# One hybrid backbone layer on one core: loads and orders of the mixer's pass and first steps rearranged, the first hyena half of the output projection put between the first scores and the first numerators

## The chip, the cores and the metric

The kernel runs on one core of one Trainium2 chip. The metric is the device time of one execution in microseconds, the median of several executions. The core has five engines with queues of their own: PE (TensorE, matrix products), DVE (VectorE), ACT (ScalarE), POOL (GpSimd) and SP (SyncE), which issues all the DMA transfers here. They meet at semaphores only.

## The reference

One layer (DEPTH = 1) over 2048 latent tokens and 256 context tokens of width 1024. A modulated, normalised input is projected; one half of the width feeds a bidirectional mLSTM with 4 heads of 128, the other a Hyena operator with long filters. Both are gated, joined and sent through one output projection:

```
shift, scale, gate = split(silu(c) @ w_mod + b_mod)
h = rms_norm(x, pre_gain) * (1 + scale) + shift
qk, v, o, zm, g, hy, zh = split_proj(h @ w_in)
h_m = mlstm_bidirectional(...)           # scan over chunks of 64, forward and backward
m   = mlstm_output(h_m, o, zm, mh_gain)  # sigmoid(o), rms norm per head, silu(zm)
y_h = hyena_mixer(hy, zh, ...)           # two long convolutions by FFT, silu(zh)
y   = concat([m, y_h]) @ w_out
out = x + gate * rms_norm(y, post_gain)
```

## The kernel before

Three blocks follow one another: `project` (modulation and input projection, up to about 700 us), `hyena` (filters and long convolutions of four groups of 128 channels, to 1271 us) and `mixer` (to the end). All products are in float32; the large ones are done as three products of a high part (`w_hi`) and a low part (`w_lo`), and the parts are formed by ACT (high) and DVE or POOL (low). The order on every engine is written out by hand, and semaphores tie the engines together.

**The opening of `project`.** PE multiplies eight chunks of w_mod (line 501), two chunks to a row of the modulation. ACT copies a row out of PSUM (line 690, `take_mod`) and PE turns it into columns (line 492, `turn_mod`). Turn 0 stands behind chunk 2, turn 1 behind chunk 4, turns 2 and 3 behind chunk 7. When all four are done, DVE and ACT form `mod` and `gcol`, modulate the first tokens, and split the first weight tile; then PE's first projection tile (line 514) begins.

**The pass of `mixer`.** It goes over the 18 chunks of 128 tokens (NT = 18, 2 of them context). For chunk c PE turns k (`turn_k`, line 1445), ACT and DVE scale it by the forward and backward weights (`weigh_forward`, line 1559; `weigh_backward`, line 1681), and PE forms the state increments with v (`increments`, lines 1456 and 1465). DVE adds the forward ones up (`forward`, line 1692), ACT takes the backward ones out of PSUM (`take_backward`, line 1566). k and v lie in four slots. Behind both loads of a slot stands one semaphore, `kv_in`, and PE waits for it ahead of turning k; SP loads a slot again when the increments of the chunk four back are done. PE's order is turn k of c+1, then increments of c. Between these loads SP issues other loads: y of the Hyena half (`yh`), rows of the first two steps (`mb`), output gates `og` and `zg`, the row `gate`. In chunks 2 to 9 ACT forms the high part of one row of w_out a chunk (`high_wo`), in the order 0 to 7; DVE makes the low parts of 0 to 3 (mlstm half), POOL those of 4 to 7 (hyena half). In the last four chunks ACT does the exponentials of step 0: `weights` (line 1602) and `inter` (line 1596).

**The steps.** 16 steps n go over the latent chunks from the last to the first. In a step PE does the scores (line 1484, k by q), the numerators (lines 1524 and 1525), the turn of y (line 1533) and two halves of the output projection into one accumulator `acc`: the hyena half (`out_hyena`) and the mlstm half (`out_mlstm`), 24 products of 512 columns each (lines 1491 to 1493). POOL covers the rows by the mask (`cover`, line 1374), scales q (`scale_q`) and applies the gates (`gates`); ACT does exponentials, squares and high parts of y (`high_hyena`, `high_mlstm`); DVE multiplies scores by weights (`products`, line 1753), forms the heads (`heads_out`, lines 1733 to 1743), the low parts of y, the backward state (`backward`, line 1718) and the results. `cover(n)` waits for all loads of step n and for the products of step n-1. Numerators n wait for the heads of step n-1. A hyena half n > 0 waits until DVE has taken the accumulator of step n-1 (`z_ready`, line 1786); that waits for ACT's squares of it (`out_squares`, line 1620), which stand on ACT behind the first `weights` of step n+2. PE's order at the start is: scores 0, numerators 0, scores 1, hyena half 0, numerators 1, turn of y 0, scores 2, mlstm half 0, numerators 2, turn of y 1, hyena half 1, scores 3 and so on.

Of the kernel before, what the change touches and what calls it, by code (L numbers as in the profile page):

```python
# [164 lines left out]
def project(nc, d, s, svec, ident, hidden, opening):  # L165

    with ExitStack() as ctx:  # L167
# [309 lines left out]
        def _(pe):  # L477
# [19 lines left out]
            for c in range(N_MOD):  # L497
# [10 lines left out]
                if c in (2, 4):  # L508
                    turn_mod(c // 2 - 1)
            turn_mod(2)  # L510
# [579 lines left out]
HIGH_WO = (2, 3, 4, 5, 6, 7, 8, 9)  # L1090

class Early:

    def __init__(self, nc, ctx, base):
# [8 lines left out]
        self.gain = at("gain", [P, HEADS], 20352)  # L1105
        self.raw_offset = base + X_AT
        self.raw = at("wo_raw", [P, KD, D], X_AT)
        self.kv_in = [sem(f"kv_in{i}") for i in range(SLOTS)]
        self.wc_in = sem("wc_in")
        self.mpb_in = sem("mpb_in")  # L1110
# [4 lines left out]
    def load_kv(self, sp, s, c):  # L1115
        slot = c % SLOTS
        sp.dma_start(self.kq[:, slot], s["k"][c]).then_inc(self.kv_in[slot], 16)
        sp.dma_start(self.v1[:, slot, :, 0:DH], s["v"][c].rearrange("p (h v) -> p h v", h=HEADS))\
          .then_inc(self.kv_in[slot], 16)

    def load(self, sp, d, s):

        self.load_kv(sp, s, 0)
        sp.dma_start(self.cols[:, :, :, :].rearrange("p d w r -> p (d w r)"), s["cols"]).then_inc(self.cols_in, 16)
        for dr in range(2):
            sp.dma_start(self.wc[:, dr, :], spread(s["small"][dr, 3])).then_inc(self.wc_in, 16)
        self.load_kv(sp, s, 1)
# [4 lines left out]
        self.load_kv(sp, s, 2)  # L1132
        self.load_kv(sp, s, 3)
        sp.dma_start(self.mask[:, :, :], d["mask"]).then_inc(self.mpb_in, 16)
        for dr in range(2):
            sp.dma_start(self.mpb[:, dr, :], spread(s["small"][dr, 2])).then_inc(self.mpb_in, 16)

def mixer(nc, d, s, out, ident, early):

    with ExitStack() as ctx:  # L1141
# [9 lines left out]
        og = sb("og", [P, 2, HEADS, P])  # L1151
        zg = sb("zg", [P, 2, HEADS, P])
        gate = sb("gate", [P, D])
        gains = sb("gains", [P, HEADS])
# [5 lines left out]
        power = sb("power_m", [P, 2, HEADS])  # L1160
        power_o = sb("power_o", [P, 2])
        mb = sb("mb", [P, 2, 2, HEADS, P])
# [12 lines left out]
        raw, mask, gain = early.raw, early.mask, early.gain  # L1175
        cols, mpb, wc = early.cols, early.mpb, early.wc
# [16 lines left out]
        gate_in = sem("gate_in_m")  # L1193
# [5 lines left out]
        kv_in = early.kv_in  # L1199
# [14 lines left out]
        first_rows_in = sem("first_rows_in")  # L1214
# [55 lines left out]
        def _(sp):  # L1270
            def load_kv(c):
                sp.wait_ge(uf_ready, c - SLOTS + 1)
                sp.wait_ge(ub_ready, backward_done(c - SLOTS))
                early.load_kv(sp, s, c)

            def load_rows(n):
                b, t = n % 2, lat(n)
                for dr in range(2):
                    src = s["rows"][dr].rearrange("(h c) t -> c h t", h=HEADS)
# [43 lines left out]
            for c in range(SLOTS, NT):  # L1323
# [5 lines left out]
                if c == 7:  # L1329
                    load_rows(1)  # L1330
# [1398 lines left out]
```

## Time and profile before

| | |
|---|---|
| median of three runs | 1599.39 us (1598.91 to 1602.81) |
| profiled execution, its own time | 1599.17 us |
| its span | 1597.4 us |
| PE busy | 1532.2 us (96%) |
| DVE, ACT, POOL busy | 691.2, 633.5, 311.7 us |
| mixer's pass | 1271.8 to 1322.6 us |
| steps | 1322.6 us to the end |

The span is the profiled part of one execution; 1.8 us of that execution's time lie around it. A row of the timeline gives start and length in microseconds, engine and line, the operation, what is written and what is read, and how many instructions are merged in it; in brackets stands how long the engine was idle before it, and what released it.
### The profile page before, as it was taken

How to read it: one execution, taken by the hardware profiler on the slowest of the kernel's cores; microseconds unless marked ns; L12 is line 12 of the kernel's file. 1: busy time of each engine (PE TensorE's matmuls, PEld its weight loads, DVE VectorE, ACT ScalarE, POOL GpSimd, SP SyncE). 2: the span in 40 equal slices, each digit the busy share in tenths (PEclk: the TensorE clock that was granted, in tenths of full speed). 3: DMA queues.
4: the chain of work that ended last, by engine and by line, in shares of the span. 5: the costliest groups of instructions: out<-in, count | busy, mean ns of one | idle time of the engine just before them, and what ended most of it. 6: DMA issues, size and time to landing. Idle time of an engine off the chain costs nothing. (4 is left out here: it accounts for less than half of the span.)

```text
span 1597.4 us, 22990 instructions
## 1 busy us (share of the span) xinstructions
PE 1532.2 (96%) x8892; PEld 1344.4 (84%) x8892; DVE 691.2 (43%) x1129; ACT 633.5 (40%) x1357; POOL 311.7 (20%) x298
## 2 busy tenths in 40 slices
PE   4899999999999999999999999999999887999997
PEld 2788888888888888888888899999999776888886
DVE  1654430233333333000020377777765477555553
ACT  2785312343222222122111355445454385555551
POOL 1652000000000000000000031211213136666661
PEclk8899999999999999999999999999999899999999
DMA  8342621222222222112122464656446494666651
GB/s 345 102 125 71 234 74 56 77 73 73 79 72 74 77 72 80 71 46 99 53 77 73 169 172 123 185 136 181 111 106 157 173 270 139 199 196 196 201 185 53
DMA packets 128276, 201.92 MB, mean 126 GB/s; under 512 B 12571, under 2 KB 75793, under 8 KB 121270
## 3 DMA queue, kind: packets, MB, share of 16 engines
q1 hardware_dynamic: 128182, 200.64, 40.0%
q8 instruction: 62, 1.02, 0.3%
q14 instruction: 32, 0.26, 0.1%
HBM read 122.57 MB, written 52.86 MB: 110 GB/s over the span
## 5 line engine op out<-in xcount | busy, mean ns | idle before, releaser
L514 PE MATMUL bank<-h_hi,w_hi 128*128 128x512 f32 (+1 forms) x800 | 310.9, 389 | 11.7 <-DVE w_lo L848 9.7
L516 PE MATMUL bank<-h_hi,w_lo 128*128 128x512 f32 (+1 forms) x800 | 309.0, 386 | 0.0
L515 PE MATMUL bank<-h_lo,w_hi 128*128 128x512 f32 (+1 forms) x800 | 308.9, 386 | 0.0
L514 PEld LDWEIGHTS bank<-h_hi,w_hi 128*128 128x128 f32 x800 | 151.4, 189 | 42.1 <-ACT w_hi L654 9.8
L516 PEld LDWEIGHTS bank<-h_hi,w_lo 128*128 128x128 f32 x800 | 151.4, 189 | 30.1
L515 PEld LDWEIGHTS bank<-h_lo,w_hi 128*128 128x128 f32 x800 | 151.5, 189 | 29.6 <-issue 0.2
L912 DVE SCALAR_TENSOR_TENSOR work<-work,coef 128x504 f32<-128x504 f32 (+1 forms) x84 | 63.2, 753 | 237.2 <-ACT work L674 237.1
L514 PE MATMUL bank<-w_hi,h_hi 128*128 128x512 f32 (+1 forms) x448 | 164.5, 367 | 0.0
L515 PE MATMUL bank<-w_lo,h_hi 128*128 128x512 f32 (+1 forms) x448 | 164.1, 366 | 0.0
L516 PE MATMUL bank<-w_hi,h_lo 128*128 128x512 f32 (+1 forms) x448 | 164.1, 366 | 0.0
L664 ACT ACTIVATE work<-bank 128x512 f32<-128x512 f32 (+1 forms) x72 | 40.4, 562 | 296.8 <-PE bank L516 296.8
L2129 POOL MEMSET ones_h<- 128x128 f32 x1 | 0.2, 206 | 758.2 <-POOLq L167 758.2
L672 ACT COPY work<-bank 128x512 f32<-128x512 f32 (+1 forms) x84 | 48.3, 575 | 231.1 <-PE bank L516 231.1
L848 DVE TENSOR_TENSOR w_lo<-stage,w_hi 128x2048 fp32r<-128x2048 f32 x18 | 41.3, 2292 | 216.7 <-ACT w_hi L654 214.1
L2137 POOL TENSOR_TENSOR prod<-prod,hidden 128x512 f32<-128x512 f32 x48 | 61.3, 1277 | 277.1 <-DVE hidden L2522 277.1
L1491 PE MATMUL acc<-wo_hi,y_hi 128*128 128x512 f32 x256 | 103.7, 405 | 7.1 <-DVE late L1786 5.0
L1493 PE MATMUL acc<-wo_hi,y_lo 128*128 128x512 f32 x256 | 100.9, 394 | 0.0
L1492 PE MATMUL acc<-wo_lo,y_hi 128*128 128x512 f32 x256 | 100.9, 394 | 0.0
L514 PEld LDWEIGHTS bank<-w_hi,h_hi 128*128 128x128 f32 x448 | 84.5, 189 | 15.2 <-ACT work L664 0.9
L515 PEld LDWEIGHTS bank<-w_lo,h_hi 128*128 128x128 f32 x448 | 84.5, 189 | 13.8
L516 PEld LDWEIGHTS bank<-w_hi,h_lo 128*128 128x128 f32 x448 | 84.5, 189 | 13.8
L1602 ACT ACTIVATE late<-late,cols 128x128 f32<-128x128 f32 x128 | 40.8, 392 | 68.9 <-POOL late L1374 68.9
(249 smaller groups left out, 2801.7 us busy)
## 6 DMA issues: line engine op xcount, KB each, us to landing
H<-spectrum SPq DMA_DIRECT2D x192, 128.0 KB, 2.3
stage<-in_w_in SPq DMA_DIRECT2D x18, 1024.0 KB, 5.6
s_hy<-work SPq DMA_DIRECT2D x48, 256.0 KB, 2.2
x<-s_hy SPq DMA_DIRECT2D x8, 1024.0 KB, 5.0
kq<-s_k SPq DMA_DIRECT2D x32, 256.0 KB, 4.5
v<-s_v SPq DMA_DIRECT2D x32, 256.0 KB, 5.2
mb<-s_rows SPq DMA_DIRECT2D x32, 256.0 KB, 5.6
late<-in_x SPq DMA_DIRECT2D x16, 512.0 KB, 4.8
```

Source lines behind the costliest of these rows:

```text
L514: pe.matmul(out, lhs[0], rhs[0], start=(k == 0), stop=False)
L515: pe.matmul(out, lhs[0], rhs[1], start=False, stop=False)
L516: return pe.matmul(out, lhs[1], rhs[0], start=False, stop=(k == KD - 1))
L664: act.activation(res[slot][:, 0:width], bank[slot][:, 0:width], func, bias=bias)\
L672: act.copy(raw[r][:, 0:width], bank[slot][:, 0:width]).then_inc(raw_ready, 1)
L848: dve.tensor_tensor(w_lo[:, par, :, 0:width], stage[:, par, :, 0:width], w_hi[:, par, :, 0:width].bitcast(F32), ALU.subtract).then_inc(w_l ...
L912: dve.scalar_tensor_tensor(y[:, :, 1:e], u[:, :, 0:e - 1], w_left, y[:, :, 1:e], ALU.mult, ALU.add).then_inc(tap_first, 1)
L1491: pe.matmul(o, y_hi[:, k, :], w_hi[:, k, cut], start=(k == HEADS), stop=False)
L1492: pe.matmul(o, y_hi[:, k, :], w_lo[:, k, cut], start=False, stop=False)
L1493: mm = pe.matmul(o, y_lo[:, k, :], w_hi[:, k, cut], start=False, stop=(k == HEADS - 1))
L1602: ins = act.activation(E[:, dr, hd, :], E[:, dr, hd, :], ACT.Exp, scale=-1.0, bias=column(dr, 0, lat(n) + NT_CTX, hd))
L2137: pool.tensor_tensor(cut, cut, crossed[:, t % 2], ALU.add).then_inc(added, 1)
```

## The change

In the opening, turn 2 moves ahead of chunk 7. In the pass, k and v get semaphores of their own (`k_in`, `v_in`), a slot's k is loaded again once it was turned, and PE waits for v ahead of the increments only. The rows of step 0, both first pairs of output gates and the row `gate` are loaded in `Early.load`, with a semaphore `steps_in`, ahead of the last y that the hyena block stores; they get memory of their own there. In a step's loads the rows come first. The rows of w_out are split in the order 4, 5, 6, 7, 1, 2, 3, 0, and the first backward state update stands behind chunk 13 on DVE. The cast and the low part of the first hyena y come ahead of the end of the pass and of products 0; hyena half 0 stands between scores 0 and numerators 0; the first `high_mlstm` comes ahead of the second `weights` of step 2.

```diff
-                if c in (2, 4):
+                if c in (2, 4, 6):
                     turn_mod(c // 2 - 1)
-            turn_mod(2)
             turn_mod(3)
...
-HIGH_WO = (2, 3, 4, 5, 6, 7, 8, 9)
+HIGH_WO = {2: 4, 3: 5, 4: 6, 5: 7, 6: 1, 7: 2, 8: 3, 9: 0}
+WO_NTH = {k: i + 1 for i, k in enumerate(HIGH_WO.values())}
+STEPS_IN = 160
+BACKWARD_AT = 13
...
+        for dr in range(2):
+            sp.dma_start(self.mb[:, 0, dr], rows_of(s, dr, LAST)).then_inc(self.steps_in, 16)
+        for b in range(2):
+            sp.dma_start(self.og[:, b].rearrange("p h v -> p (h v)"), s["ozh"][0, LAST - b]).then_inc(self.steps_in, 16)
+            sp.dma_start(self.zg[:, b].rearrange("p h v -> p (h v)"), s["ozh"][1, LAST - b]).then_inc(self.steps_in, 16)
+        sp.dma_start(self.gate[:, :], spread(s["gate"][0])).then_inc(self.steps_in, 16)
...
-            def load_kv(c):
+            def load_k(c):
+                sp.wait_ge(k_turned, c - SLOTS + 1)
+                early.load_k(sp, s, c)
+
+            def load_v(c):
                 sp.wait_ge(uf_ready, c - SLOTS + 1)
                 sp.wait_ge(ub_ready, backward_done(c - SLOTS))
-                early.load_kv(sp, s, c)
+                early.load_v(sp, s, c)
...
                 sp.wait_ge(num_ready, n - 1)
+                load_rows(n)
                 sp.dma_start(kT[:, slot], s["k"][t + NT_CTX]).then_inc(step_in[b], 16)
...
-                load_rows(n)
...
             def increments(c):
+                pe.wait_ge(v_in[c % SLOTS], 16 * (c // SLOTS) + 16)
...
                     scores(n)
-                if n == 1:
+                if n == 0:
                     out_hyena(0)
...
+                if c == NT - 2:
+                    high_hyena(0)
             take_backward(NT - 1)
 
-            high_hyena(0)
...
                     out_squares(n - 2)
+                if n == 1:
+                    high_mlstm(0)
                 if n + 1 < NT_LAT:
                     weights(n + 1, 1)
-                if 0 < n <= NT_LAT:
+                if 1 < n <= NT_LAT:
                     high_mlstm(n - 1)
...
+                if n == 0:
+                    low_hyena(0)
                 if n < NT_LAT:
                     products(n)
-                if n == 0:
-                    low_hyena(0)
```

On PE, in the opening, before: `bank<-stage` and `bank<-mods` are chunks of w_mod (two chunks stand in a row x16), `bank<-hidden,work` is a turn.

```order
L501 MATMUL bank<-mods,hidden 32x256 x16
L492 MATMUL bank<-hidden,work 128x2 x4
L501 MATMUL bank<-mods,hidden 32x256 x24
L492 MATMUL bank<-hidden,work 128x2 x8
L514 MATMUL bank<-h_hi,w_hi 128x256
```

and now:

```order
L501 MATMUL bank<-mods,hidden 32x256 x16
L492 MATMUL bank<-hidden,work 128x2 x4
L501 MATMUL bank<-mods,hidden 32x256 x16
L492 MATMUL bank<-hidden,work 128x2 x4
L501 MATMUL bank<-mods,hidden 32x256 x8
L492 MATMUL bank<-hidden,work 128x2 x4
L513 MATMUL bank<-h_hi,w_hi 128x256
```

One of the two turns behind the last chunk stands ahead of it.

On PE, from the first scores (`psS<-kq`) on, before; `psN<-v,late` and `psN<-CF` or `CB` are numerators, `acc` is the output projection:

```order
L1484 MATMUL psS<-kq 128x128 x4
L1524 MATMUL psN<-v_57,late 128x129
L1525 MATMUL psN<-CF,wib 128x129
...
L1484 MATMUL psS<-kq 128x128 x4
L1491 MATMUL acc<-wo_hi,y_hi 128x512
L1492 MATMUL acc<-wo_lo,y_hi 128x512
L1493 MATMUL acc<-wo_hi,y_lo 128x512
```

and now, from the same scores on:

```order
L1502 MATMUL psS<-kq 128x128 x4
L1509 MATMUL acc<-wo_hi,y_hi 128x512
L1510 MATMUL acc<-wo_lo,y_hi 128x512
L1511 MATMUL acc<-wo_hi,y_lo 128x512
...
L1542 MATMUL psN<-v_57,late 128x129
L1543 MATMUL psN<-CF,wib 128x129
```

The 24 products of the hyena half, which stood behind the second scores, stand behind the first ones, ahead of all numerators.

On DVE, at the end of the pass, before; `CF` is the forward sum, `CB` the backward update, `late<-psS` the products, `y_lo` the low part of y:

```order
L1681 TENSOR_TENSOR kw<-psY,cols 128x512
L1692 SCALAR_TENSOR_TENSOR CF<-CF,wc,psN 128x129 x4
L1718 SCALAR_TENSOR_TENSOR CB<-CB,wc 128x129 x4
L1753 TENSOR_TENSOR late<-psS,late 128x512 x2
L1765 TENSOR_TENSOR y_lo<-yh,y_hi 128x512
L1718 SCALAR_TENSOR_TENSOR CB<-CB,wc 128x129 x4
L1733 SCALAR_TENSOR_TENSOR den<-psN,cols 128x8
```

and now:

```order
L1700 TENSOR_TENSOR kw<-psY,cols 128x512
L1711 SCALAR_TENSOR_TENSOR CF<-CF,wc,psN 128x129 x4
L1783 TENSOR_TENSOR y_lo<-yh,y_hi 128x512
L1771 TENSOR_TENSOR late<-psS,late 128x512 x2
L1728 SCALAR_TENSOR_TENSOR CB<-CB,wc 128x129 x4
L1751 SCALAR_TENSOR_TENSOR den<-psN,cols 128x8
```

The first backward update left this place, and the low part of y went ahead of the products.

## Rows read from the trace of the kernel before

**Rows 1.** Timeline of PE, the opening (start us, length us, line, tiles, count, [idle])

```profile
22.04 1.05 PE L492 MATMUL bank<-hidden,work 128*128 128x2 f32 x8
...
26.06 1.07 PE L501 MATMUL bank<-mods,hidden 128*32 128x256 f32 x16 [1.47 <-DMA mods<-in_w_mod]
28.55 1.94 PE L501 MATMUL bank<-mods,hidden 128*32 128x256 f32 x16 [1.42 <-DMA mods<-in_w_mod]
30.42 3.58 PE L492 MATMUL bank<-hidden,work 128*128 128x2 f32 x16
43.73 0.55 PE L514 MATMUL bank<-h_hi,w_hi 128*128 128x256 f32 x1 [9.73 <-DVE w_lo L848]
```

**Rows 2.** Timeline of ACT, then of DVE, the opening

```profile
30.56 0.59 ACT L690 COPY work<-bank 128x512 f32<-128x512 f32 x1 [5.32 <-PE bank L501]
...
34.11 0.26 DVE L872 TENSOR_TENSOR mod<-bank,bmod 128x16 f32<-128x16 f32 x2 [21.65 <-PE bank L492]
```

**Rows 3.** Waits, pass, 1271 to 1322 us (who, on what: total us, times, longest)

```profile
PE psS L1445 <- DMA v<-s_v: 5.9, 5, 2.3
```

**Rows 4.** Timeline of PE, end of the pass and first scores

```profile
1316.15 0.66 PE L1445 MATMUL psS<-ident,kq 128*128 128x128 f32 x4 [2.30 <-DMA v<-s_v]
...
1322.56 1.06 PE L1484 MATMUL psS<-kq 128*128 128x128 f32 x8
```

**Rows 5.** Timeline of ACT, end of the pass

```profile
1311.67 0.59 ACT L1566 COPY CB<-psN 128x516 f32<-128x516 f32 x1 [0.59 <-PE psN L1465]
...
1314.75 1.11 ACT L1559 ACTIVATE kw<-psY,cols 128x128 f32<-128x128 f32 x4
...
1320.86 0.59 ACT L1566 COPY CB<-psN 128x516 f32<-128x516 f32 x1 [0.46 <-PE psN L1465]
```

**Rows 6.** Timeline of DVE, the first steps

```profile
1326.37 5.21 DVE L1718 SCALAR_TENSOR_TENSOR CB<-CB,wc 128x129 f32<-128x129 f32 x4
...
1333.90 1.28 DVE L1753 TENSOR_TENSOR late<-psS,late 128x512 f32<-128x512 f32 x2
...
1349.73 1.13 DVE L1718 SCALAR_TENSOR_TENSOR CB<-CB,wc 128x129 f32<-128x129 f32 x4
```

**Rows 7.** Timeline of PE, the first steps behind the scores

```profile
1325.90 0.49 PE L1524 MATMUL psN<-v,late 128*128 128x129 f32 x2 [2.29 <-DVE late L1753]
...
1329.58 1.06 PE L1484 MATMUL psS<-kq 128*128 128x128 f32 x8
1330.39 0.48 PE L1491 MATMUL acc<-wo_hi,y_hi 128*128 128x512 f32 x1
...
1335.97 0.38 PE L1524 MATMUL psN<-v,late 128*128 128x129 f32 x2
...
1339.97 0.66 PE L1533 MATMUL psY<-ident,kw 128*128 128x128 f32 x4 [0.28 <-DVE kw L1774]
...
1343.61 0.50 PE L1491 MATMUL acc<-wo_hi,y_hi 128*128 128x512 f32 x1 [2.09 <-DVE y_lo L1758]
...
1356.83 0.76 PE L1491 MATMUL acc<-wo_hi,y_hi 128*128 128x512 f32 x1 [3.23 <-DVE late L1786]
```

**Rows 8.** Timeline of POOL, covering of steps 1 and 3

```profile
1325.93 2.93 POOL L1374 TENSOR_TENSOR late<-mb,mask 128x512 f32<-128x512 f32 x2 [1.96 <-DVE late L1753]
...
1352.14 2.49 POOL L1374 TENSOR_TENSOR late<-mb,mask 128x512 f32<-128x512 f32 x2 [1.16 <-DMA mb<-s_rows]
```

**Rows 9.** Windows: busy us by engine, granted PE clock, DMA share, GB/s

```profile
30.00:32.00 2.00, 2.00 (x16) 1.58 (x8) 0.00 (x0) 0.59 (x1) 0.00 (x0) 0.50 1.03 416
1252.00:1271.00 19.00, 16.04 (x99) 14.78 (x97) 6.77 (x10) 5.86 (x10) 3.71 (x3) 0.73 0.10 26
1357.00:1363.00 6.00, 6.00 (x15) 4.65 (x16) 4.15 (x10) 3.63 (x15) 3.34 (x4) 0.50 0.62 203
```

**Rows 10.** Waits of PE from 1357 to 1560 us

```profile
PE acc L1491 <- DVE late L1786: 3.2, 1, 3.2
```

**Rows 11.** DMA issues, 1200 to 1360 us: size, median us to landing

```profile
v<-s_v SPq DMA_DIRECT2D x20, 256.0 KB, 4.8
```

More of the change, by code:

```diff
@@ L1089, with rows_of @@
 SLOTS = 4
-HIGH_WO = (2, 3, 4, 5, 6, 7, 8, 9)
+HIGH_WO = {2: 4, 3: 5, 4: 6, 5: 7, 6: 1, 7: 2, 8: 3, 9: 0}
+WO_NTH = {k: i + 1 for i, k in enumerate(HIGH_WO.values())}
+STEPS_IN = 160
+BACKWARD_AT = 13
+def rows_of(s, dr, t):
+    src = s["rows"][dr].rearrange("(h c) t -> c h t", h=HEADS)
+    return spread(src[t + NT_CTX:t + NT_CTX + 1].rearrange("c h t -> (c h) t"))
 class Early:
@@ L1105, in __init__ @@
         self.gain = at("gain", [P, HEADS], 20352)
+        self.gains = at("gains", [P, HEADS], 20448)
+        self.power = at("power_m", [P, 2, HEADS], 20384)
+        self.power_o = at("power_o", [P, 2], 20416)
         self.raw_offset = base + X_AT
         self.raw = at("wo_raw", [P, KD, D], X_AT)
-        self.kv_in = [sem(f"kv_in{i}") for i in range(SLOTS)]
-        self.wc_in = sem("wc_in")
-        self.mpb_in = sem("mpb_in")
+        self.og = at("og", [P, 2, HEADS, P], X_AT + 32768)
+        self.zg = at("zg", [P, 2, HEADS, P], X_AT + 36864)
+        self.gate = at("gate", [P, D], X_AT + 40960)
+        self.mb = at("mb", [P, 2, 2, HEADS, P], X_AT + 45056)
+        self.k_in = [sem(f"k_in{i}") for i in range(SLOTS)]
+        self.v_in = [sem(f"v_in{i}") for i in range(SLOTS)]
+        self.steps_in = sem("first_steps_in")
         self.cols_in = sem("cols_in")
@@ L1113, in __init__, with load_k, load_v @@
         self.y_out = sem("y_out_h")
-    def load_kv(self, sp, s, c):
+    def load_k(self, sp, s, c):
         slot = c % SLOTS
-        sp.dma_start(self.kq[:, slot], s["k"][c]).then_inc(self.kv_in[slot], 16)
+        sp.dma_start(self.kq[:, slot], s["k"][c]).then_inc(self.k_in[slot], 16)
+    def load_v(self, sp, s, c):
+        slot = c % SLOTS
         sp.dma_start(self.v1[:, slot, :, 0:DH], s["v"][c].rearrange("p (h v) -> p h v", h=HEADS))\
-          .then_inc(self.kv_in[slot], 16)
+          .then_inc(self.v_in[slot], 16)
     def load(self, sp, d, s):
-        self.load_kv(sp, s, 0)
+        self.load_k(sp, s, 0)
+        self.load_v(sp, s, 0)
         sp.dma_start(self.cols[:, :, :, :].rearrange("p d w r -> p (d w r)"), s["cols"]).then_inc(self.cols_in, 16)
         for dr in range(2):
-            sp.dma_start(self.wc[:, dr, :], spread(s["small"][dr, 3])).then_inc(self.wc_in, 16)
-        self.load_kv(sp, s, 1)
+            sp.dma_start(self.wc[:, dr, :], spread(s["small"][dr, 3])).then_inc(self.cols_in, 16)
+        self.load_k(sp, s, 1)
+        self.load_v(sp, s, 1)
         sp.dma_start(self.gain[:, :], d["gaincol"]).then_inc(self.wo_in, 16)
@@ L1150, in mixer @@
         sb("raw_m", [P, KD * D])
[L1151 to L1154, printed above, removed]
+        sb("steps_m", [P, 3 * D])
+        sb("mb_m", [P, 2 * D])
         den = sb("den", [P, 2, HEADS])
@@ L1175, in mixer @@
         raw, mask, gain = early.raw, early.mask, early.gain
+        og, zg, gate, mb = early.og, early.zg, early.gate, early.mb
+        gains, power, power_o = early.gains, early.power, early.power_o
         cols, mpb, wc = early.cols, early.mpb, early.wc
@@ L1720, in backward @@
                 ins.then_inc(cb_ready, 1)
-            backward(0, NT_LAT)
+            for c in range(NT):
+                if c != 2:
+                    weigh_backward(c)
+                if c:
+                    forward(c - 1)
+                if HIGH_WO.get(c - 1, KD) < HEADS:
+                    low_wo(HIGH_WO[c - 1])
+                if c == BACKWARD_AT:
+                    backward(0, NT_LAT)
             def heads_out(n):
```

77 lines of the change are left out of this document (27 added, 50 removed).

## The prediction

> **What bounds the kernel now.** I read the page first: PE is busy in nearly every slice, so a microsecond is worth something only where PE waits. The waits of PE then fall into four places. In the opening PE waits for the chunks of w_mod, turns two rows of the modulation at the end, and then stands 9.73 us until the first weights are ready [rows 1]. Everything between is one chain: DVE had waited 21.65 us for the last turned row [rows 2]. In the mixer's pass PE waits 5 times, 5.9 us together, for the v of a chunk, the last time 2.30 us [rows 3, 4]. In the first steps it waits 2.29, 0.28, 2.09 and 3.23 us [rows 7]. From 1357 to 1560 us the waits of PE hold one entry, and that is the 3.23 us wait which ends at 1356.83 [rows 10]. So from there on the kernel is PE alone, and whatever time the start of the second hyena half (1356.83) gains or loses is kept to the end. The sum therefore is: how much earlier does that matmul start, and at which clock. I write T for the start of the first scores, 1322.56 before [rows 4].
>
> **Part 1, the turn of modulation row 2 goes ahead of the last chunk.** Chunk 6 is done at 26.06 + 1.07 = 27.13, chunk 7 starts at 28.55 when its data lands, and the two turns behind it take 3.58 us, 1.79 each [rows 1], at a granted clock of 0.50, the level of 1.2 GHz [rows 9]. ACT's copy that turn 2 needs was over at 30.56 - 5.32 = 25.24 [rows 2]. So turn 2 fits into PE's wait for chunk 7: at the pace of the earlier turn (1.05 us [rows 1]) it ends at 28.2, and no matmul is added or lost. Behind chunk 7 only the copy (0.59 us) and turn 3 remain. If PE keeps the pace of 26.06 (1.07 us a chunk), chunk 7 ends at 29.62, the copy at 30.28, turn 3 at about 31.4 instead of 34.0: 2.6 us earlier. If the clock falls as before, chunk 7 ends at 30.49, the copy at 31.15, turn 3 at 31.15 + 0.07 + 1.79 = 33.0: 1.0 us. I take 2.6: the earlier turn, with a chunk ahead of and behind it, ran at 1.05 and the chunk at 26.06 still at 1.07; the fall came in the one wait that had no turn in it. What follows on DVE and ACT is a chain of work, and the first tile at 43.73 waits for the end of it, so I carry the 2.6 through. The end that takes it away again is a weight tile whose load is late, which no row excludes: 0 is the lower bound, 2.6 plus some 0.4 of a cold first tile that warms earlier the upper.
>
> **Part 2, the pass.** Three things move. (a) k and v have semaphores of their own, a slot's k is loaded again as soon as it was turned, and v is waited for only by its own increments. A v needs 4.8 us to land and its issue 0.5 [rows 11]; so far PE needs it behind two steps of 2.23 us (4.5 us after the slot is free), from now on behind three and a turn (7.1 us). That takes the cause of the waits away. (b) Rows, o and z gates and the output gate, 2 MB with 7 issues on SP, go from the pass to the stretch behind the last hyena group. There DMA is busy a tenth of 19 us at 26 GB/s [rows 9], and nothing on SP's queue behind them is due until the y of the last group at 1271. I price them at nothing; without that cover they would cost the pass what they cost now. (c) The rows of W are split in another order (hyena half first, so that POOL begins at chunk 2), DVE's low parts come four chunks later, and one backward state update moves from the end to chunk 13.
>
> Not all 5.9 us come back. At the end the turn could run at 1313.85 instead of 1316.15, but the increments behind it need ACT's scaling of 1314.75, which is 3.08 us behind the take of 1311.67: take, first load of the Exp table, four Exp and only then the scaling [rows 5]. That stretch stays. Of the last wait about 0.7 us is real, 1.6 is ACT's. Of the four earlier waits (5.9 - 2.3 = 3.6 us) I keep about half: in chunks 2 to 9 ACT's step (four scalings, a take, a row of W) is an estimated 2.5 us against PE's 2.23, and DVE's with a low part about 2.8, now in chunks 7 to 10. Walking chunk by chunk, the take of 1311.67 comes near 1309.85, that of 1320.86 near 1318.9, T near 1320.6: **2.0 us earlier**. Bounds: 0 (ACT is the bound at every chunk) and 3.6. The cast of the first y goes between two of ACT's last tasks, 0.5 us, where ACT had 0.46 idle ahead of the take [rows 5]; I count it in the 2.0.
>
> The moved state update is the place for a rule. Four such instructions took 5.21 us at 1326.37 while POOL covered (2.93 us for a pair from 1325.93), and 1.13 us at 1349.73 [rows 6, 8]. The Trainium skill (SBUF — State Buffer, "SBUF: two separate sides") says that a VectorE operation with two SBUF inputs and a GpSimd one that reads SBUF take an exclusive lock in turn; the trace agrees with 5.21 against 1.13. By that rule chunk 13 is a gain only if POOL's first cover is over by then; beside it DVE would be some 1 us late and the pass gain 1.4 instead of 2.0. I have the cover end at about 1307.4 and the update begin at 1308.7, and leave 2.0.
>
> **Part 3, the first steps.** Before: scores, wait 2.29, numerators 0 (1325.90 to 1329.58, 3.7 us), scores 1 (0.8), the hyena half (1330.39 to 1335.97, 5.6 us), numerators 1 without a wait [rows 7]. Now the hyena half stands between the first scores and the first numerators. Its operands are there: the cast is done before T, DVE's low part precedes the products. It ends at T + 0.8 + 5.6 = T + 6.4, numerators 0 at T + 10.1 (before T + 7.0). Behind them DVE forms the heads, which it could not start before 1326.37 + 5.21 = 1331.58 (T + 9.0), held by the update; it was ready for the products at 1333.90 = T + 11.3 [rows 6]. Now the update is over by T + 7.5 even at 5.21 us, the heads take 2.4 from T + 10.1, products 1 begin at T + 12.5: **1.2 us later**, not 3.1. PE meanwhile stands still from T + 10.9 to about T + 13.9, because the hyena half that used to fill this place is gone: a new wait of 3 us for the removed 2.29.
>
> The lag of 1.2 passes through gates and roots to the turn of y (before T + 17.4, now 18.6), and to the mlstm half at 1343.61 = T + 21.05. There 0.5 is won back, because ACT now casts y before its second Exp group: T + 21.75. The next and deciding point is the second hyena half. It waits for the output squares, which stand on ACT behind the Exp group of step 3, and that behind POOL's cover, which waited 1.16 us for rows of DMA [rows 8]. Rows are now the first of the step's loads, but they are issued about 1.2 later with the rest: I put the cover at T + 29.2 to T + 30.7 (before T + 29.6) and take **0.4 us later** than before relative to T, between -0.4 and +1.1. So 1356.83 becomes 1356.83 - 2.6 - 2.0 + 0.4 = 1352.6.
>
> **Sum.** The profiled execution took 1599.17, 1.8 over its span of 1597.4 and 0.2 under the median of 1599.39. 1599.2 - 2.6 - 2.0 + 0.4 = **1595.0 us**, if PE's clock behaves as before.
>
> **The clock** is the open term. In 1357 to 1363 the granted clock was 0.50 [rows 9], after the 3.23 us wait; 15 matmuls took 6.0 us there, at the pace of 1335.97 - 1330.39 = 5.58 for 24 they take 3.5. That stretch costs about 2.5 to 3 us, on the path. The new order has waits of about 3.0 (T + 10.9), 1.8 (T + 20) and 2.5 to 3 us (T + 31.6) in its place.
>
> **Rivals.**
> A (chance 0.43), the forecast: one half-clock stretch still falls on the second hyena half. 1594 to 1596.5.
> B (0.27), the clock falls at T + 10.9 instead, slows numerators 1, and the second hyena half then starts after a wait under 2 us at 2.4 GHz. Numerators 1 have slack towards that start, so 3 us come back: 1592.0. For it: the wait of 3 us is as long as the one that was followed by the fall. Against it: waits of 2.29 and 2.30 were not followed by one, and the difference is small.
> C (0.15), the fall comes at T + 10.9 and again at the mlstm half or the second hyena half: 2.5 us more, 1597.5.
> D (0.10), the pass gains nothing, because ACT bounds it or v still lands late behind k of the next chunk: 1597.
> E (0.05), slower. The place is scores 1: the hyena half ahead of numerators 0 delays heads, y and the mlstm half. If numerators 0 are 3.3 late (5.58 - 2.29) and nothing is given back, and numerators 1 and the mlstm half both run at half clock (2.5 and 3.0 us), the steps lose 8.8; it decides once this loss passes the 4.6 that opening and pass gain. With the opening at 1.0 and the pass at 1.0: 1599.2 - 2.0 + 8.8 = 1606.
> That the loads still arrive as before, since each is issued behind the same semaphores of the increments (the change not doing what it says), is D with the opening's gain alone.
>
> **Chances.** A difference under 0.3%, 4.8 us, can't be told from none. Faster by more (below 1594.6) takes B and about four tenths of A: 0.44. Slower by more (above 1604.2): 0.05. The rest 0.51. The range 1591.0 to 1598.5 holds A, B, most of C and D.
>
> **What the profile would show.** Part 1: two turns of about 1.05 us, one ahead of chunk 7, and the first tile at 41.1. Part 2: no PE wait for v, first scores at 1318.0 (T less the opening's 2.6). Part 3: a PE wait of about 3 us between scores 1 and numerators 1, products 1 at T + 12.5, the mlstm half at T + 21.8, the second hyena half at T + 34.3 to 35.4. Wrong I would be by a clock that falls elsewhere, or by a load in the first steps that lands later than its turn in the queue lets me think.

## The result, and the profile after

The changed kernel takes 1606.16 us (median of 7 runs, 1602.73 to 1608.65) against 1598.91 (1593.12 to 1602.81, 7 runs) before: a ratio of 1.0043 (95% interval 1.0028 to 1.0059). It is 0.4% slower. The forecast was 1595.0 us with a range of 1591.0 to 1598.5; both are missed, on the other side of no change. The profiled execution of after took 1602.73 us, with a span of 1601.0. It is the fastest of its seven, so its span shows 3.6 us of the 7.3 that the medians differ by.

Up to the fourth scores the changed kernel does better than forecast. Timeline of PE in the pass and the first steps, after; it answers to [rows 4] and [rows 7] (here and below, a row at the edge of the window that was asked for shows fewer instructions than there are, such as x5 for x8):

```profile
1318.14 1.06 PE L1502 MATMUL psS<-kq 128*128 128x128 f32 x8
1318.95 0.48 PE L1509 MATMUL acc<-wo_hi,y_hi 128*128 128x512 f32 x1
...
1324.66 0.39 PE L1542 MATMUL psN<-v,late 128*128 128x129 f32 x2
...
1328.23 1.06 PE L1502 MATMUL psS<-kq 128*128 128x128 f32 x8
1332.18 0.80 PE L1542 MATMUL psN<-v,late 128*128 128x129 f32 x2 [2.89 <-DVE late L1771]
...
1340.59 0.50 PE L1509 MATMUL acc<-wo_hi,y_hi 128*128 128x512 f32 x1 [1.85 <-DVE y_lo L1776]
...
1358.47 0.72 PE L1502 MATMUL psS<-kq 128*128 128x128 f32 x5
```

T is now 1318.14; before it was 1322.56. The second hyena half starts at 1352.78, behind a wait of 0.76 on DVE, against 1356.83 before, and the fourth scores stand at 1358.47 against 1365.30: 6.8 us ahead. The waits of PE from 1357 to 1560 us, which were nothing but the end of one wait before [rows 10], now read (who, on what: total us, times, longest):

```profile
PE acc L1509 <- DVE late L1804: 3.4, 7, 0.9
```

And the 16th scores, before and then after, in the timeline of PE:

```profile
1555.55 0.72 PE L1484 MATMUL psS<-kq 128*128 128x128 f32 x5
```

```profile
1558.30 0.94 PE L1502 MATMUL psS<-kq 128*128 128x128 f32 x7
```

Twelve steps took 1555.55 - 1365.30 = 190.25 us before, 15.85 each, and 1558.30 - 1358.47 = 199.83 after, 16.65 each (from 16.16 to 17.34). The lead of 6.8 us is spent, and 2.8 more. The spans add up as follows: up to the start of the pass 0.75 us less (1271.83 and 1271.08), the pass 3.67 less (50.73 and 47.06), T to the fourth scores 2.41 less (42.74 and 40.33), twelve steps 9.58 more, the rest 0.85 more (41.85 and 42.70). Sum: 3.60, the difference of the spans.

Not all of the 6.8 us is the change's. The fourth scores stand at T + 42.74 in the profiled execution of before, but at T + 40.06 to 40.45 in three kernels below that have its code unchanged up to there (before_shift32, opening_only, rows_first_alone), and at T + 39.9 to 41.9 with the hyena half moved. So the 2.41 us between T and the fourth scores are mostly luck of one pair of executions: the half-clock stretch on the second hyena half [rows 9] was about twice as long in before as in before_shift32 and opening_only, and in after none fell on it.

**What the steps show.** First, the products of the output projection are slower. Groups of instructions of PE from 1400 to 1550 us, before and then after (line, operation, count, busy us, mean ns, idle before):

```profile
L1491 PE MATMUL acc<-wo_hi,y_hi 128*128 128x512 f32 x150 | 60.1, 401 | 0.0
L1493 PE MATMUL acc<-wo_hi,y_lo 128*128 128x512 f32 x150 | 58.5, 390 | 0.0
L1492 PE MATMUL acc<-wo_lo,y_hi 128*128 128x512 f32 x149 | 58.0, 389 | 0.0
```

```profile
L1509 PE MATMUL acc<-wo_hi,y_hi 128*128 128x512 f32 x144 | 58.5, 406 | 3.1 <-DVE late L1804 2.9
L1511 PE MATMUL acc<-wo_hi,y_lo 128*128 128x512 f32 x144 | 57.1, 396 | 0.0
L1510 PE MATMUL acc<-wo_lo,y_hi 128*128 128x512 f32 x144 | 57.1, 396 | 0.0
```

Each is 5 to 7 ns longer at the same granted clock, 1.00 over these 150 us in both. A half of 24 takes 5.70 us instead of 5.55, two of them make 0.3 us a step. The tiles, shapes and order are the same; what differs is that `gains`, `power_m` and `power_o` left the mixer's own memory, 96 B a partition, so that by the program's memory plan `wo_hi` (and `wo_lo` 32 KB behind it) starts at byte 92000 of a partition instead of 92096.

Second, PE waits for `late` of DVE L1804, the product that frees the accumulators. Timeline of one step of after, SP's queue, then POOL, ACT and DVE:

```profile
1420.74 0.34 SPq L1343 DMA_DIRECT2D out<-late  x1
1421.12 0.43 SPq L1338 DMA_DIRECT2D late<-in_x  x1
1421.60 1.48 SPq L1306 DMA_DIRECT2D mb<-s_rows  x2
1423.12 0.51 SPq L1317 DMA_DIRECT2D kq<-s_k  x1
1423.67 0.43 SPq L1318 DMA_DIRECT2D kq<-s_q  x1
1424.14 0.53 SPq L1319 DMA_DIRECT2D v<-s_v  x1
...
1430.90 2.50 POOL L1390 TENSOR_TENSOR late<-mb,mask 128x512 f32<-128x512 f32 x2 [1.97 <-DMA v<-s_v]
...
1432.21 1.28 ACT L1618 ACTIVATE late<-late,cols 128x128 f32<-128x128 f32 x4 [5.84 <-POOL late L1390]
1433.39 0.57 ACT L1636 ACTIVATE kw<-acc 128x512 f32<-128x512 f32 x1
...
1434.16 1.29 DVE L1804 TENSOR_TENSOR late<-acc,gate 128x512 f32<-128x512 f32 x2 [4.51 <-ACT kw L1636]
...
1435.90 1.28 DVE L1811 SCALAR_TENSOR_TENSOR late<-late,root_o 128x1024 f32<-128x1024 f32 x1 [0.45 <-POOL root_o L1425]
```

This is a ring: a chain of waits that leads back to its own start one step later. The store of a step is followed on SP by the x load and the loads of a later step; the cover waits for the last of these loads; ACT's weights wait for the cover, the output squares (L1636) stand right behind them, then DVE's product, the residual, and at 1437.22 the next store. From cover to store it takes 6.32 us; from store to cover it took 10.16 here, in the mean of 12 steps 10.34, with the 6.32 together 16.66, the 16.65 of the steps. None of it is PE's. Before, in the same places (timeline of SP and POOL of before):

```profile
1439.50 0.34 SPq L1321 DMA_DIRECT2D out<-late  x1
1439.88 0.43 SPq L1316 DMA_DIRECT2D late<-in_x  x1
1440.36 0.78 SPq L1293 DMA_DIRECT2D kq<-s_k  x1
1441.18 0.50 SPq L1294 DMA_DIRECT2D kq<-s_q  x1
1441.73 0.53 SPq L1295 DMA_DIRECT2D v<-s_v  x1
1442.30 1.17 SPq L1280 DMA_DIRECT2D mb<-s_rows  x2
...
1448.74 2.80 POOL L1374 TENSOR_TENSOR late<-mb,mask 128x512 f32<-128x512 f32 x2 [1.29 <-DMA mb<-s_rows]
```

The cover stood 9.24 us behind the store here, 9.52 in the mean of 12 steps (8.77 to 10.78). With 6.32 behind it, the time from cover to store where PE does not hold it up, that makes 15.84, as long as PE's own step. That they agree to the hundredth is chance: with the rows last and the loads behind the store, the five other kernels below have 9.33 to 9.79, so rings of 15.65 to 16.11. But the ring had next to no slack before the change either.

The change made it longer than the step, with the very edit that was to shorten it: one semaphore counts all five loads of a step, so the cover, which reads the rows alone, waits for whichever lands last. That is now v: it needs 6.8 us to land (5.2 before), while the rows need 5.7 in either order. Landing times of v from 1400 to 1550 us (count, size, median us from issue to landing), before and then after:

```profile
v<-s_v SPq DMA_DIRECT2D x9, 256.0 KB, 5.2
```

```profile
v<-s_v SPq DMA_DIRECT2D x9, 256.0 KB, 6.8
```

Why v lands later in the last place than rows do I can't say from these traces.

### The profile page after: what moved, and what is told of

The parts are those of the page before. It is cut to its first block and busy times, and to the rows that moved or that the text cites. A ratio compares the mean times of both kernels' runs of the same rounds, so it can differ in the third digit from the quotient of the medians.

```text
span 1601.0 us, 22986 instructions
## 1 busy us (share of the span) xinstructions
PE 1538.2 (96%) x8892; PEld 1342.6 (84%) x8892; DVE 687.4 (43%) x1129; ACT 630.4 (39%) x1357; POOL 313.1 (20%) x298
## 5 line engine op out<-in xcount | busy, mean ns | idle before, releaser
L513 PEld LDWEIGHTS bank<-h_hi,w_hi 128*128 128x128 f32 x800 | 151.5, 189 | 41.9 <-ACT w_hi L653 9.8
```

What stands on the lines that cost most here:

```text
L513: pe.matmul(out, lhs[0], rhs[0], start=(k == 0), stop=False)
```

## The experiments

Each kernel was timed beside runs of before on the same chip; ratios are to those, with their 95% intervals. "Step" is the mean of the 12 steps from the fourth to the 16th scores, "half" the start of the second hyena half and "fourth" that of the fourth scores, both in us from T; "cover behind store" is the mean time from a store's issue to the next cover over 12 steps. All but the medians and ratios come from one profiled execution of each kernel.

| kernel | median us | ratio | half | fourth | step | cover behind store |
|---|---|---|---|---|---|---|
| before | 1598.91 | | 34.27 | 42.74 | 15.85 | 9.52 |
| after | 1606.16 | 1.0043 (1.0028 to 1.0059) | 34.64 | 40.33 | 16.65 | 10.34 |
| rows_last | 1602.69 | 1.0008 (0.9993 to 1.0023) | 34.68 | 41.92 | 16.15 | 9.64 |
| shift_back | 1604.06 | 1.0027 (1.0014 to 1.0040) | 34.68 | 41.85 | 16.52 | 10.33 |
| both_back | 1598.32 | 0.9989 (0.9974 to 1.0004) | 34.65 | 40.22 | 16.13 | 9.79 |
| before_shift32 | 1604.13 | 1.0020 (1.0004 to 1.0036) | 33.24 | 40.45 | 16.11 | 9.72 |
| loads_ahead | 1594.55 | 0.9979 (0.9964 to 0.9994) | 34.37 | 41.52 | 15.84 | 5.91 |
| after_loads_ahead | 1600.00 | 1.0012 (1.0003 to 1.0022) | 34.58 | 40.27 | 16.15 | 6.06 |
| hyena_back | 1592.22 | 0.9965 (0.9951 to 0.9978) | 31.23 | 38.39 | 15.84 | 9.55 |
| opening_only | 1599.39 | 1.0011 (0.9999 to 1.0023) | 33.19 | 40.08 | 15.84 | 9.33 |
| rows_first_alone | 1609.26 | 1.0060 (1.0047 to 1.0073) | 34.53 | 40.06 | 16.63 | 10.32 |
| hyena_back_ahead | 1591.82 | 0.9954 (0.9939 to 0.9968) | 31.21 | 36.77 | 15.84 | 5.92 |
| rows_own_count | 1601.10 | 1.0017 (1.0007 to 1.0026) | 34.23 | 39.93 | 16.15 | 8.35 |
| own_count_hyena_back | 1591.14 | 0.9950 (0.9935 to 0.9965) | 31.22 | 38.40 | 15.84 | 8.42 |

**The two suspects, taken back one by one.** rows_last is the changed kernel with the rows behind v again:

```diff
                 sp.wait_ge(num_ready, n - 1)
-                load_rows(n)
                 sp.dma_start(kT[:, slot], ...)
...
                   .then_inc(step_in[b], 16)
+                load_rows(n)
```

> The changed kernel with one thing undone: in a step's loads the rows come last again, as before. Up to the fourth scores the changed kernel was 6.8 us ahead of the one before, and from there to the end it lost 10.4 us, at 16.3 to 17.3 us a step against 15.84. Theory of the loads: covering waits for all loads of a step; with v as the last of them they land later, and the loop store, loads, cover, weights, squares, gate, result, store is longer than PE's own work of a step. It expects no waits of PE for the gated accumulator between the second hyena half and the last steps, and a step of about 16.1 us (15.84 plus 0.3 for slower products, next theory), so about 1599 us. Rival, the shifted weights: the halves of the projection take 5.70 instead of 5.55 us, and the waits follow from that; then the waits stay and the time stays near 1605.

It came to 1602.69 where I expected about 1599; by its ratio of 1.0008 that is 1600.2 beside a before of 1598.91. Its steps came to exactly 16.15 without a wait of PE: what is left over 15.84 is the products, still 406 and 397 ns. shift_back is the changed kernel with a pad of 96 B, which puts `wo_hi` back at 92096:

```diff
         sb("mb_m", [P, 2 * D])
+        sb("pad_w", [P, 24])
```

> The changed kernel with 96 bytes of padding a partition ahead of wo_hi, so that wo_hi, wo_lo, CF and CB start at the same address as in the kernel before (92096 instead of 92000, a multiple of 64 instead of only 32); nothing else. Theory of the shift: the address makes the 512-column products slower. It expects the halves back at 5.55 us from 5.70. The loop of the loads stays as it is, so by the theory of the loads the step stays at 16.3 to 17 us with longer PE waits, and the time near 1605 us. If the slow products are the cause of all, the step falls to 15.84 and the time to 1596.

1604.06. The three groups of products are at 400, 390 and 390 ns again and the first two steps take 15.84, but from the third on they take 16 to 17.5 and PE waits up to 1.47 us: the ring binds whatever PE's own step is. So neither edit alone gives back its full share, since the other bound is close below. both_back has both:

> The changed kernel with both undone: rows last and the 96 bytes of padding. If the two theories together hold the whole loss, the step is 15.84 us with no PE wait, and the gains of opening, pass and first steps stay: 4 to 7 us under the kernel before, about 1593. If something else slows the steps, the step stays above 15.84.

1598.32, level with before and not the 1593 that I expected if the two causes were all. Its steps are uneven, 15.84 to 16.94, with three waits of 0.58 to 0.89, although the rows are last. The address by itself, a pad of 32 B ahead of `wo_hi` in the kernel before (92128):

```diff
         mb = sb("mb", [P, 2, 2, HEADS, P])
+        sb("pad_w", [P, 8])
```

> The kernel before with 32 bytes of padding ahead of wo_hi (92128, no multiple of 64) and nothing else. Theory of the shift: halves 5.70 us instead of 5.55, a step 0.3 us longer, 15 steps, so 4 to 5 us slower, about 1603. Rival (the products are slower for another reason, such as transfers at the same time): no change, 1599.

Groups of PE from 1400 to 1550 us in before_shift32:

```profile
L1492 PE MATMUL acc<-wo_hi,y_hi 128*128 128x512 f32 x151 | 61.3, 406 | 0.0
L1494 PE MATMUL acc<-wo_hi,y_lo 128*128 128x512 f32 x151 | 59.6, 395 | 0.0
L1493 PE MATMUL acc<-wo_lo,y_hi 128*128 128x512 f32 x150 | 59.3, 396 | 0.0
```

All its steps take 16.11 against 15.84, and no work was moved. The address costs 0.27 us a step and 3.2 us of the whole by the ratio (1.0020). The pad moves all that lies behind it too, `CF` and `CB` among it, but the 128x129 products that read these stay at 275 ns here and in before.

**Is it the ring?** Here the loads of step n+2 leave it: they are issued ahead of the store, in both_back (loads_ahead) and in the changed kernel itself (after_loads_ahead):

```diff
             for n in range(NT_LAT + 2):
+                if n == 1:
+                    load_step(2)
                 if 0 < n < LAST:
-                    load_step(n + 1)
                     load_fin(n + 1)
                     load_yh(n + 1)
+                if 0 < n < LAST - 1:
+                    load_step(n + 2)
                 if n >= 2:
                     store(n - 2)
```

> The changed kernel with the step's rows last and the 96 B pad ahead of wo_hi, and one edit more: the loads of step n+2 are issued ahead of the store and the x load of the step, not behind them. Nothing is left out. Theory (loop of loads): without this edit the steps are uneven, 15.84 to 16.94 us, because store, x, loads, cover, weights and squares form a ring that is itself about as long as PE's 15.84. The loads then leave that ring, so every step is 15.84 us, no PE wait in the steps over 0.3 us behind the second hyena half, and the time is 4 us under the same kernel without it: about 1594.5. Rival (clock): the uneven steps come from a granted clock that falls, whatever the loads do: steps stay uneven, 1598.

> The changed kernel itself with only that edit: loads of step n+2 are issued ahead of the store and of x. Rows stay first, wo_hi stays at its new address. Nothing is left out. Theory (two causes that add up: the ring of loads and the address of wo_hi): the waits of PE for the output's accumulators go, the slower products stay, so steps are 16.1 us each and even; 12 steps take 193.5 instead of 200.0, and the time is 1600. Rival (the rows, being first, delay v and with it something else than the ring): waits of PE stay, steps of 16.3 to 17.3, 1606.

1594.55 and 1600.00, as the ring has it. The cover stands 6 us behind the store, every step is 15.84 in the one and 16.15 in the other, and PE never waits. The difference of the two is 5.4 us in the medians. The address makes 0.31 x 12 = 3.7 of it in the twelve steps, and more in the halves outside them; but the two differ in the place of the rows as well, so the rest isn't separated. And the rows' order alone, in the kernel before:

```diff
                 sp.wait_ge(num_ready, n - 1)
+                load_rows(n)
                 sp.dma_start(kT[:, slot], ...)
...
-                load_rows(n)
```

> The kernel before with one line moved: in the loads of a step the rows are issued first and v last. wo_hi keeps its address, no work moves. Nothing is left out. Theory (ring of store, x load, step loads, cover, weights, squares, residual, store): with rows first this ring took 16.65 us a step in the changed kernel and 16.66 in the one with the pad, whatever PE's own step was. PE starts here with the lead that its half-clock stretch leaves it (about 2.9 us), and loses 0.8 a step from it: no PE wait in the first three or four steps, waits of up to 1.5 us after, the 12 steps from the fourth scores take 190.1 + 12 x 0.81 - 2.9 = 197, so the end is 7 us later: about 1604. Rival (the order of the loads costs nothing by itself; the waits come only from the moved hyena half that takes PE's lead): steps of 15.84, 1598.

One moved line makes the kernel 1609.26, 0.6% slower, at least as much as the whole change (the intervals of the two ratios overlap from 1.0047 to 1.0059). Waits of PE from 1360 to 1560 us in rows_first_alone:

```profile
PE acc L1491 <- DVE late L1786: 6.6, 9, 1.4
```

The mean step is 16.63, as the ring says (10.32 + 6.31). My expectation was 5 us too low, since I gave PE a lead of 2.9 us over the ring that it did not have: the second hyena half ran here at full clock, and the scores of PE followed the store at the closest distance seen (3.9 us) from the first step on. That also fits both_back, with 3.9 to 4.0 us from the start. In before, PE was slowed by the half-clock stretch behind the 3.23 us wait [rows 9], and its scores followed the store at 6.9 us at first, at 3.9 to 5.5 later: that distance paid for the ring's late steps (up to 10.78 us to the cover). Where PE has no such distance, each late step of the ring is a wait. hyena_back below has the loads and the address of both_back, starts at 5.6 us, and has no wait.

**The count.** In rows_own_count the rows come first as in the changed kernel, but are counted on semaphores of their own:

```diff
-                    pool.wait_ge(step_in[b], steps_in(n))
+                    pool.wait_ge(rows_in[b], rows_count(n))
...
-                    act.wait_ge(step_in[b], steps_in(n))
+                    act.wait_ge(rows_in[b], rows_count(n))
```

> The changed kernel with the rows of a step counted apart from k, q and v: POOL's cover and ACT's first Exp group wait for the rows alone, PE's scores and POOL's products with q wait for k, q and v. Rows stay first, wo_hi stays at its new address, the hyena half stays moved. Nothing is left out. Theory (rows first costs time because one semaphore counts all loads of a step, so that the cover waits for v, which is now last): rows are issued 0.9 to 2.0 us behind the store and land 5.7 later, so the cover starts 7 to 8 us behind the store and not 10.35; the ring is about 14 us, below PE's 16.15, PE does not wait from the second hyena half to the end of the steps, steps are 16.15, and the time is 1600. Rival (the DMA queues are the bound, whatever is waited for): the cover stays at 9.5 or more behind the store, steps stay uneven, 1603 to 1606.

1601.10, steps of 16.15. Waits of POOL from 1400 to 1550 us, after and then rows_own_count:

```profile
POOL late L1390 <- DMA v<-s_v: 20.6, 9, 2.8
```

```profile
POOL late L1394 <- DMA mb<-s_rows: 0.2, 1, 0.2
```

The 20.6 us are gone with the order of the loads unchanged, so it was the count that made the order expensive. The Trainium skill (DMA: Bandwidth & Descriptors, "Queues, rings and completion order") says that a DMA's increment of its semaphore lands only after every earlier write of the same DMA engine. No run here tests that, since a wait for the count of all five loads waits for v with or without it. What the trace shows of after is that k needs 5.7 us, q 5.9 and v, the last issued, 6.8.

**The moved hyena half** goes back behind the second scores on PE, in both_back, in loads_ahead and in rows_own_count with the pad:

```diff
                 if n < NT_LAT:
                     scores(n)
-                if n == 0:
+                if n == 1:
                     out_hyena(0)
```

> The changed kernel with rows last and the pad, and the first hyena half back behind the second scores on PE. Nothing is left out. Tells what the moved half is worth by itself. By the prediction's steps: between first scores and first numerators the wait of about 2.3 us is back, the one of 3 us between second scores and second numerators is gone; the second hyena half starts within 1 us of T + 34.7, so the fourth scores stand at T + 40 to 41 as without this edit (1361.85 - 1321.63 = 40.2), and the time is 1598 as there. Rival (the moved half is what brings the first steps forward): the fourth scores come at T + 42.7 as before the change, 1600.5.

> The changed kernel with rows last, the pad ahead of wo_hi, the first hyena half back behind the second scores, and the loads of step n+2 issued ahead of the store. Nothing is left out. Theory: the ring has already ceased to hold PE where the half-clock stretch gave it a lead (12 steps of 15.84 without this edit), so the loads ahead bring nothing more: steps of 15.84, fourth scores at T + 38.4, 1592. Rival (the ring, or v that lands late, still costs time in the first steps): the second hyena half starts earlier than T + 31.2 and the time is 1590.

> The same separate count of rows, with the 96 B pad ahead of wo_hi and the first hyena half back behind the second scores. Nothing is left out. Theory: all three causes are gone, rows stay first: steps of 15.84 without waits, the second hyena half at T + 31 or earlier, and 1592, as with the loads ahead (1591.82). Rival: rows first still costs something: above 1596.

1592.22, 1591.82 and 1591.14. This I had wrong: the second hyena half starts at T + 31.2 in all three, and at T + 34.2 to 34.7 with the half moved. Timeline of DVE in hyena_back, and then in after:

```profile
1324.55 4.20 DVE L1729 SCALAR_TENSOR_TENSOR CB<-CB,wc 128x129 f32<-128x129 f32 x4
1329.30 0.69 DVE L1758 TENSOR_TENSOR kw<-psN,den 128x512 f32<-128x512 f32 x1
...
1331.06 1.28 DVE L1772 TENSOR_TENSOR late<-psS,late 128x512 f32<-128x512 f32 x2
```

```profile
1320.44 4.26 DVE L1728 SCALAR_TENSOR_TENSOR CB<-CB,wc 128x129 f32<-128x129 f32 x4
...
1330.84 1.28 DVE L1771 TENSOR_TENSOR late<-psS,late 128x512 f32<-128x512 f32 x2
```

Products 1 begin at 1331.06 - 1322.25 = T + 8.8 with the half back, at 1330.84 - 1318.14 = T + 12.7 with it moved, and stood at T + 11.3 before [rows 6]. The 2.5 us between T + 11.3 and T + 8.8 are DVE's: one state update and the low part of y left the place ahead of products 1, and the update that stayed took 4.20 us instead of 5.21; no run separates these. The moved half costs 3.9, because heads, y and everything behind them wait for numerators 0. Between loads_ahead and hyena_back_ahead, which differ in nothing else, that is 3.2 us at the second half, and 4.0 by the ratios (0.9979 and 0.9954). The spread of the second half over kernels with the same order up to there is up to 1.3 us (33.19 to 34.53 with the code of before), so the 3 us stand clear of it. The fourth scores of hyena_back_ahead came at T + 36.8 and not at the expected 38.4, since its half-clock stretch fell ahead of the second hyena half. The three kernels are faster than before by 0.35 to 0.5%, and so faster than both kernels that were given.

**The opening** alone, in the kernel before:

```diff
-                if c in (2, 4):
+                if c in (2, 4, 6):
                     turn_mod(c // 2 - 1)
-            turn_mod(2)
```

> The kernel before with only the first part of the change: the turn of modulation row 2 stands ahead of the last chunk of w_mod. Nothing is left out. Prediction's term: 2.6 us earlier at the first tile (41.1) and at the end, 1596.3. By the trace of the changed kernel, where the clock fell to 0.50 ahead of the last two chunks and the turns took 1.87 each: the first tile at 44 to 45, nothing gained, 1599.

1599.39, no gain. Timeline of PE in the opening, opening_only; it answers to [rows 1]:

```profile
24.18 1.07 PE L501 MATMUL bank<-mods,hidden 128*32 128x256 f32 x16 [1.17 <-DMA mods<-in_w_mod]
26.51 1.93 PE L501 MATMUL bank<-mods,hidden 128*32 128x256 f32 x16 [1.26 <-DMA mods<-in_w_mod]
28.37 1.87 PE L492 MATMUL bank<-hidden,work 128*128 128x2 f32 x8
30.17 1.93 PE L501 MATMUL bank<-mods,hidden 128*32 128x256 f32 x16
32.81 1.86 PE L492 MATMUL bank<-hidden,work 128*128 128x2 f32 x8 [0.70 <-ACT work L689]
44.40 0.55 PE L513 MATMUL bank<-h_hi,w_hi 128*128 128x256 f32 x1 [9.72 <-DVE w_lo L847]
```

The clock had fallen before the turn: chunk 6 already runs at 1.93. At that pace the turn no longer fits into the wait for chunk 7 but pushes it from 28.55 to 30.17, and the last turn ends at 34.7, not at 34.0.

## Why the prediction was wrong, by its own steps

**What bounds the kernel: wrong, and this decided it.** "So from there on the kernel is PE alone, and whatever time the start of the second hyena half (1356.83) gains or loses is kept to the end." Of the two claims the first was read rightly from [rows 10]: PE did not wait. The second does not follow. That PE waits for nothing says that PE is the longest, not by how much. The ring beside it had 9.52 us from store to cover in the mean, with 6.32 behind it 15.84, which is PE's step. So nothing could lengthen it without a loss, and the change did: 16.65 a step, 9.6 us more over twelve steps, the slower products included. I had its trace in hand, even cited a cover that waited 1.16 us for its rows [rows 8], and never added store to store. It has cost 4 to 6 us in the changed kernel (1606.16 against 1600.00 and 1601.10 with the loads or the count mended; by the ratios 4.2 to 5.0).

**Rows first: priced in the first steps only.** "Rows are now the first of the step's loads" stood there as a help. In the loop it was a loss of 0.8 us a step, 0.6% by itself (rows_first_alone). The order of issue matters to a waiter only through the last increment that it counts, and that was in the code.

**The address of `wo_hi`: no term at all.** Of what moved to `Early` I priced the transfers only ("I price them at nothing"), and never asked where the rest of the memory would lie. It cost 0.3 us a step: 3.2 us by itself in before_shift32, 3.0 between rows_last and both_back (ratios of 1.0008 and 0.9989), and 2.6 beside the long ring, which hides a part of it (1.0043 and 1.0027 for after and shift_back).

**Part 1, 2.6 us: fell.** The first tile is at 44.83 after and was forecast at 41.1; it was at 43.73 before, so this execution lies even 1.1 us outside the lower bound of 0. In the time of the whole kernel the part alone is worth nothing (1.0011, 0.9999 to 1.0023). The failed step is the choice of pace: I took the turn at 1.05 us since the chunk ahead of it had run at 1.07 in that one execution; in the executions of after and of opening_only chunk 6 ran at half clock. In one profiled execution, that of own_count_hyena_back, the turn did run at 1.05, and the first tile was at 42.79; but rows_first_alone, with the turns in the old place, had both in 1.95 together and its first tile at 42.38. So what pays there is the clock, and no run shows that the place of the turn sets it.

**Part 2, 2.0 us: right in kind, too small.** No PE wait for v is left. The pass takes 47.06 us in after and 50.73 before: 3.7 us, just over the upper bound of 3.6 that I had set for it. I halved what the four earlier waits would give because of ACT's load, and that was the term too small: they went whole. At the end it was as I had it: the increments wait 1.68 us at 1311.71 for ACT's scaling. The size is no single number either: over all profiled executions the pass takes 50.7 to 54.3 us in the four kernels with the old pass and 47.1 to 48.8 in the ten with the new one. T came at 1318.14 where I said 1318.0, by luck, since the terms are others: 0.75 and 3.67 instead of 2.6 and 2.0, and the 0.75 is no part of the change (the pass began anywhere from 1270 to 1277 us in the profiled executions, whichever kernel it was). The rule on the shared port (the Trainium skill, SBUF — State Buffer, "SBUF: two separate sides") held at the place where I weighed it: the update at chunk 13, with POOL's cover over since 1303.7, took 1.14 us, and the next one, beside a cover, 4.26.

**Part 3, 0.4 us later: right as a sum, wrong as a judgement.** The wait between scores 1 and numerators 1 is 2.89 (3 forecast), products 1 stand at T + 12.7 (12.5), the mlstm half at T + 22.45 (21.8), the second hyena half at T + 34.64 (34.67 as the sum has it), at 1352.78 where I said 1352.6. But the sum of a good edit (3 us) and a bad one (3.4) hid that the kernel had a better form.

**The clock.** It fell at numerators 1, as rivals B and C have it, again in the mlstm half, as C has it, and not at the second hyena half, as B has it. Windows of after (length, busy us of the engines, granted clock, DMA share, GB/s):

```profile
1332.00:1336.00 4.00, 3.82 (x21) 3.82 (x22) 2.99 (x6) 1.28 (x8) 2.97 (x5) 0.61 0.66 222
1340.00:1348.00 8.00, 7.41 (x26) 5.91 (x27) 4.12 (x8) 4.16 (x18) 6.57 (x6) 0.79 0.69 221
1353.00:1359.00 6.00, 6.00 (x29) 4.90 (x29) 4.15 (x10) 3.63 (x15) 3.37 (x3) 1.00 0.64 215
```

The mlstm half took 7.25 us instead of 5.70, but C's 2.5 us more did not come of it: the second hyena half behind it waited for DVE even so (0.76 us). rows_last, shift_back and loads_ahead show C's other form, a fall at numerators 1 and at the second hyena half, with the fourth scores at T + 41.5 to 41.9 instead of 39.9 to 40.3. So which of B and C comes differs with the execution. B's price fits the fourth scores, 6.8 us ahead, but in part by the luck named above; the ring took it back, and the less PE lags behind the store, the more of the ring's late steps it feels, as both_back shows. Rival E ended at 1606, the time that was measured, but by a loss of 8.8 us in the first steps, which isn't there. Its number is a coincidence.

## What to carry to other kernels

Where an engine is busy without a wait, measure the length of every ring that runs beside it, store to store, before an edit that gains a microsecond is carried to the end. A ring as long as the step has no slack: here the order of one queue's loads lengthened it by 0.8 us a step, and the gain was gone within the steps. When loads share one semaphore, to issue the one that is needed first ahead of the others does not help it; give it a count of its own. After any edit of the memory plan, compare the mean duration of the operations that were not touched.

## What the runs showed of the hardware that I had not expected

- The start of the moving tile counts. With `wo_hi` at byte 92096 of a partition the three groups of 128x512 products take 401, 390 and 389 ns in the mean, at 92000 and at 92128 they take 406 and 395 to 397, at the same clock. 92096 is a multiple of 64, the other two of 32 alone; no other residue was tried, and the pad moves `wo_lo` too, so that the rule in terms of 64 is only the simplest that fits.
- A 256 KB load of v in the last place of the five needs 6.8 us to land (after), in the place before the rows 5.2 (before); rows need 5.7 first or last.
- From one profiled execution to the next, the start of the pass differs by up to 7 us (1269.8 in opening_only, 1277.1 in before_shift32), more than most terms of my sum; only times counted from T could be compared.
